# Partition sums by a high and a low fp32r product instead of one fp32 product, in a two-block transformer kernel

## What is computed

```python
def rmsnorm(x, w):                       # HGRN2: o of each head, 128 wide
    y = x32 * lax.rsqrt(jnp.mean(x32 * x32, axis=-1, keepdims=True) + EPS)

def l2norm(x):                           # GDN: q and k of each head
    return x * lax.rsqrt(jnp.sum(x * x, axis=-1, keepdims=True) + EPS)

# stick breaking: -log_stay is softplus(z), masked
later = lax.cumsum(log_stay, axis=3, reverse=True) - log_stay
weights = jnp.where(valid, jnp.exp(log_beta + later), 0.0)
```

## Time and profile before

| | us |
|---|---|
| median of 3 runs | 2780.7 (2780.24 to 2782.86) |
| profiled execution | 2784.13 |
| its span, first to last instruction | 2782.3 |
| PE busy | 2749.6 |
| VectorE busy | 1959.7 |
| ScalarE busy | 1325.1 |
| GpSimd busy | 71.4 |

### The profile page before, as it was taken

The page is one execution under the profiler, slowest core; times in us unless marked ns, Lnnn a source line. Parts: engine busy times, 40 slices in busy tenths (PEclk is TensorE's granted clock), DMA queues, the critical chain, the costliest instruction groups (busy, mean ns, idle before and its releaser), DMA issues.

```text
span 2782.3 us, 42599 instructions
## 1 busy us (share of the span) xinstructions
PE 2749.6 (99%) x15230; PEld 2370.1 (85%) x15230; DVE 1959.7 (70%) x2726; ACT 1325.1 (48%) x1656; POOL 71.4 (3%) x95
## 2 busy tenths in 40 slices
PE   8999999999999999999999999999999999999998
PEld 7888888887888888888878888888888888888887
DVE  6777777768888888644465677757578888885444
ACT  6444444435444444433365555566454444443443
POOL 0000000010000000000000000000000000000000
PEclk9999999999999999999999999999999999999999
DMA  6544444454555555665545533345455555555554
GB/s 231 173 154 163 153 159 153 153 160 149 186 190 199 186 181 189 189 191 187 189 133 175 167 130 128 123 149 184 144 180 183 192 190 181 192 193 189 187 182 151
DMA packets 132883, 479.28 MB, mean 172 GB/s; under 512 B 14720, under 2 KB 16912, under 8 KB 132640
## 3 DMA queue, kind: packets, MB, share of 16 engines
q1 hardware_dynamic: 132144, 474.15, 51.6%
q0 software_dynamic: 624, 3.53, 0.4%
HBM read 475.53 MB, written 2.10 MB: 172 GB/s over the span
## 4 chain that ended last, share of the span: by engine, by line
PE 77%; DVE 10%; issue 5%; DMA 4%; ACT 3%; DVEq 1%; ACTq 0%; SPq 0%
PE acc L397 26%; PE acc L399 13%; PE acc L420 8%; PE acc L422 8%; PE acc L421 8%; DMA raw<-stream 4%; PE acc L369 4%; DVE wts L320 4%; ACT wts L314 2%; PE ps L1209 2%; PE acc L371 2%; DVE cy L1974 2%; DVE cin L347 1%; DVE half L339 1%; PE ps L1732 1%
## 5 line engine op out<-in xcount | busy, mean ns | idle before, releaser
L397 PE MATMUL acc<-hs,wts 128*128 128x512 f32 x4672 | 1651.6, 396 | 5.2 <-DVE wts L320 2.7
L320 DVE TENSOR_TENSOR wts<-raw,wts 128x1024 fp32r<-128x1024 f32 x896 | 1069.5, 1224 | 607.3 <-ACT wts L314 607.1
L314 ACT ACTIVATE wts<-raw 128x1024 fp32r<-128x1024 f32 x896 | 921.7, 1054 | 920.3 <-PE acc L399 406.5
L399 PE MATMUL acc<-hs,wts 128*128 128x256 f32 x4672 | 1308.1, 280 | 0.0
L397 PEld LDWEIGHTS acc<-hs,wts 128*128 128x128 f32 x4672 | 879.8, 188 | 201.5 <-issue 6.8
L399 PEld LDWEIGHTS acc<-hs,wts 128*128 128x128 f32 x4672 | 880.1, 188 | 2.2 <-issue 2.2
L420 PE MATMUL acc<-wts,acts 128*128 128x512 f32 x704 | 279.1, 396 | 0.9 <-DVE wts L320 0.8
L422 PE MATMUL acc<-wts,acts 128*128 128x512 f32 x704 | 279.1, 396 | 0.0
L421 PE MATMUL acc<-wts,acts 128*128 128x512 f32 x704 | 276.7, 393 | 0.0
L328 ACT ACTIVATE half<-acc 128x512 f32<-128x512 f32 x162 | 96.1, 593 | 169.3 <-PE acc L399 150.3
L420 PEld LDWEIGHTS acc<-wts,acts 128*128 128x128 f32 x704 | 132.2, 188 | 32.9 <-DVE wts L320 2.2
(11 more groups left out here) (318 smaller groups left out, 2182.3 us busy)
## 6 DMA issues: line engine op xcount, KB each, us to landing
raw<-stream SPq DMA_DIRECT2D x896, 512.0 KB, 3.8
xf<-xT SPq DMA_DIRECT2D x4, 512.0 KB, 7.6
memr<-memT POOLq DMA_DIRECT2D x1, 2048.0 KB, 8.8
outT<-memr SPq DMA_DIRECT2D x4, 256.0 KB, 2.3
outT<-memr SPq DMA_DIRECT2D x2, 512.0 KB, 3.8
KQ<-masks POOLq DMA_DIRECT2D x1, 448.0 KB, 6.1
vec<-vecs POOLq DMA_DIRECT2D x1, 352.0 KB, 6.4
cst<-consts POOLq DMA_DIRECT2D x1, 256.0 KB, 5.9
```

Of the source, the lines that this page charges most:

```text
L314: nc.scalar.activation(whi[:, b, :], raw[:, b, :], ACT.Copy).then_inc(hi_ready, 1)
L320: nc.vector.tensor_tensor(wlo[:, b, :], raw[:, b, :], whi[:, b, :].bitcast(F32), ALU.subtract).then_inc(lo_ready, 1)
L397: nc.tensor.matmul(acc[:, 2 * par + n, :], whi[:, b, c:c + P], src[:, kt, :], start=start, stop=False)
L399: mm = nc.tensor.matmul(acc[:, 2 * par + n, 0:T], wlo[:, b, c:c + P], src[:, kt, 0:T], start=False, stop=stop)
```

## The change

Every sum named above is made by two fp32r products that add up in the accumulator, of a high part (rounded to fp32r) and a low part (the rest).

- HGRN: ScalarE squares twice, into `out_sq` and, rounded, into `sqh`. VectorE subtracts one from the other (`sql`), in a step of its own, in its third step. PE's sum goes two steps later and waits for `sql`; Ln and Exp and VectorE's scaling go one step of their engines later. `out_rms` lies where `sqh` lies.
- Stick breaking: ScalarE copies softplus, rounded (`spp[:, 0]`), VectorE subtracts (`spp[:, 1]`). The sums are in another layout: bank 0 holds the 256 columns of both heads, bank 1 the last 128 of both, so that one product serves two heads. VectorE's subtraction from `zm` becomes two instructions. All from the sums on goes one block later.
- GDN: ScalarE squares a second time, rounded (`gsh`), behind the first square and ahead of the table of Ln. VectorE subtracts (`gsl`) as the first instruction of the head's work. PE's sums go one step later and wait for that; the k by k product stays in its step.
- The constants are copied once to fp32r (`ones_r`, `sums_r`).

```diff
@@ hg_vector_out
-            yield from pause(3)
+            yield from pause(2)
+            dve.wait_ge(hg_act_out.sem, hg_act_out.count("sqh", turn))
+            nc.vector.tensor_tensor(sql, out_sq, sqh.bitcast(F32),
+                                    ALU.subtract).then_inc(hg_vec_out.sem, 1)
+            yield from pause(2)
             dve.wait_ge(hg_act_out.sem, hg_act_out.count("or", turn))
@@ hg_scalar_out
             nc.scalar.activation(out_sq, ps[:, 0, :], ACT.Square).then_inc(hg_act_out.sem, 1)
-            yield
+            nc.scalar.activation(sqh, ps[:, 0, :], ACT.Square).then_inc(hg_act_out.sem, 1)
+            yield from pause(2)
@@ hg_tensor_out
-            yield from pause(4 if last else 2)
-            pe.wait_ge(hg_act_out.sem, hg_act_out.count("osq", turn))
-            nc.tensor.matmul(ps[:, 2, :], ones, out_sq, start=True, stop=True).then_inc(hg_pe_out.sem, 1)
+            yield from pause(6 if last else 4)
+            pe.wait_ge(hg_vec_out.sem, hg_vec_out.count("sql", turn))
+            nc.tensor.matmul(ps[:, 2, :], ones_r, sqh, start=True, stop=False)
+            nc.tensor.matmul(ps[:, 2, :], ones_r, sql, start=False, stop=True).then_inc(hg_pe_out.sem, 1)
@@ sb_tensor
             yield from pause(9)
-            pe.wait_ge(sb_vec.sem, sb_vec.count("sp", t))
-            for h in range(2):
-                nc.tensor.matmul(ps[:, h, 0:T], row_ge, sp_[:, h, 0:T], start=True, stop=False)
-                nc.tensor.matmul(ps[:, h, P:T], ones, sp_[:, h, T:T + P], start=False, stop=True)
-                mm = nc.tensor.matmul(ps[:, h, T:T + P], row_ge, sp_[:, h, T:T + P], start=True, stop=True)
+            yield from pause(2)
+            pe.wait_ge(sb_vec.sem, sb_vec.count("spl", t))
+            now = ps[:, 0, :].rearrange("p (h n) -> p h n", h=2)
+            for s in range(2):
+                nc.tensor.matmul(now, sums_r[:, 1], spp[:, s, :, 0:T], start=(s == 0), stop=False)
+                nc.tensor.matmul(now[:, :, P:T], sums_r[:, 0], spp[:, s, :, T:T + P], start=False, stop=(s == 1))
+                mm = nc.tensor.matmul(ps[:, 1, 0:T], sums_r[:, 1], spp[:, s, :, T:T + P], start=(s == 0), stop=(s == 1))
@@ sb_scalar
-            yield from pause(5)
+            yield from pause(2)
+            act.wait_ge(sb_vec.sem, sb_vec.count("sp", t))
+            nc.scalar.activation(spp[:, 0], sp_[:], ACT.Copy).then_inc(sb_act.sem, 1)
+            yield from pause(4)
@@ sb_vector
-            yield from pause(3)
+            yield from pause(2)
+            dve.wait_ge(sb_act.sem, sb_act.count("sph", t))
+            nc.vector.tensor_tensor(spp[:, 1], sp_[:], spp[:, 0].bitcast(F32), ALU.subtract).then_inc(sb_vec.sem, 1)
+            yield from pause(2)
@@ gd_vector
             flat = "p a b -> p (a b)"
+            dve.wait_ge(gd_act_in.sem, gd_act_in.count("sqh", t))
+            nc.vector.tensor_tensor(gsl[:], gs[:], gsh[:].bitcast(F32), ALU.subtract).then_inc(gd_vec.sem, 1)
             dve.wait_ge(gd_pe.sem, gd_pe.count("rows", t))
@@ gd_scalar_in
             nc.scalar.activation(gs[:], gy[:, 0:2, :].rearrange("p a b -> p (a b)"), ACT.Square).then_inc(gd_act_in.sem, 1)
+            if t:
+                act.wait_ge(gd_vec.sem, gd_vec.count("q", t - 1))
+            nc.scalar.activation(gsh[:], gy[:, 0:2, :].rearrange("p a b -> p (a b)"),
+                                 ACT.Square).then_inc(gd_act_in.sem, 1)
             nc.scalar.preload_act_table(ACT.Ln)
@@ gd_tensor
-            pe.wait_ge(gd_act_in.sem, gd_act_in.count("sqk", t))
+            yield
+            pe.wait_ge(gd_vec.sem, gd_vec.count("sql", t))
...
             for b in range(2):
-                mm = nc.tensor.matmul(ps[:, b, :], ones, gs[:, b * 2 * T:(b + 1) * 2 * T], start=True, stop=True)
+                part = slice(b * 2 * T, (b + 1) * 2 * T)
+                nc.tensor.matmul(ps[:, b, :], sums_r[:, 0], gsh[:, part], start=True, stop=False)
+                mm = nc.tensor.matmul(ps[:, b, :], sums_r[:, 0], gsl[:, part], start=False, stop=True)
             mm.then_inc(gd_pe.sem, 1)
...
-            yield from pause(4)
+            yield from pause(3)
             pe.wait_ge(gd_vec.sem, gd_vec.count("k", t))
```

More of the change, by code:

```diff
@@ L158, in build @@
             KM = sb("KM", [P, 2, 2 * T], F32, st)
-            osr = sb("osr", [P, 2, 2 * T], F32, st)
+            out_sq = sb("out_sq", [P, 2 * T], F32, st)[:]
+            with ExitStack() as st2:
+                out_rms = sb("out_rms", [P, 2 * T], F32, st2)[:]
+            sqh = sb("sqh", [P, 2 * T], F32R, st)[:]
+            sql = sb("sql", [P, 2 * T], F32R, st)[:]
+            ones_r = sb("ones_r", [P, P], F32R, st)[:]
             AD = sb("AD", [P, 4, P], F32, st)
@@ L172, in build @@
             tls = sb("tls", [P, 2, DT, 16], F32R, st)
+            sums_r = sb("sums_r", [P, 2, P], F32R, st)
             with ExitStack() as st2:
@@ L179, in build @@
                 svn = sb("svn", [P, 4, P], F32, st2)
+                spp = sb("spp", [P, 2, 2, 384], F32R, st2)
             with ExitStack() as st2:
                 gy = sb("gy", [P, 3, 2 * T], F32, st2)
-                gs = sb("gs", [P, 4 * T], F32, st2)
-                gr = sb("gr", [P, 4 * T], F32, st2)
+                with ExitStack() as st3:
+                    gs = sb("gs", [P, 4 * T], F32, st3)
+                    gr = sb("gr", [P, 4 * T], F32, st3)
+                gsl = sb("gsl", [P, 4 * T], F32R, st2)
+                gsh = sb("gsh", [P, 4 * T], F32R, st2)
                 vb = sb("vb", [P, 4, P], F32, st2)
@@ L266, in build @@
         hg_pool = Steps(sem("hg_pool"), names("k0 k1 k2 k3 k4 k5 k6"))
-        hg_act_out = Steps(sem("hg_act_out"), names("osq oln or"))
+        hg_act_out = Steps(sem("hg_act_out"), names("osq sqh oln or"))
         hg_vec = Steps(sem("hg_vec"), names(
@@ L270, in build @@
             "lo5 up5 c4 w6 lo6 up6 c5 lo7 up7 c6"))
-        hg_vec_out = Steps(sem("hg_vec_out"), names("og os hi lo"))
+        hg_vec_out = Steps(sem("hg_vec_out"), names("sql og os hi lo"))
         hg_pe = Steps(sem("hg_pe"), names("diag g0 g1 g2 g3 g4 g5 g6 l128"))
@@ L279, in build @@
         gt_pe = Steps(sem("gt_pe"), names("both lg cum"))
-        sb_act = Steps(sem("sb_act"), names("abs e l w hi"))
-        sb_vec = Steps(sem("sb_vec"), names("zm sp w lo"))
+        sb_act = Steps(sem("sb_act"), names("abs e l sph w hi"))
+        sb_vec = Steps(sem("sb_vec"), names("zm sp spl w0 w lo"))
         sb_pe = Steps(sem("sb_pe"), names("z cs o"))
-        gd_act_in = Steps(sem("gd_act_in"), names("silu sqk"))
+        gd_act_in = Steps(sem("gd_act_in"), names("silu sqk sqh"))
         gd_act = Steps(sem("gd_act"), names(
@@ L288, in build @@
         gd_vec = Steps(sem("gd_vec"), names(
-            "d k q Tm TT nl0 nl tt0 at0 at qd t0 t1 tt1 t2 tt2 t3 tt3 t4 tt4 t5 tt5 tt6 S"))
+            "sql d k q Tm TT nl0 nl tt0 at0 at qd t0 t1 tt1 t2 tt2 t3 tt3 t4 tt4 t5 tt5 tt6 S"))
         gd_pool = Steps(sem("gd_pool"), names("z1 z2 z3 z4 z5 z6"))
@@ L959, in first_vector @@
                                   KQ[:].rearrange("p a b -> p (a b)")[:, 0:LEVELS * P])
+            dve.wait_ge(cst_in, 16)
+            nc.vector.tensor_copy(ones_r, ones)
             yield
@@ L1138, in hg_vector @@
                 yield
-        out_sq, out_rms = osr[:, 0], osr[:, 1]
         def hg_vector_out(dve, turn, par):
             n = hin[:, par]
-            yield from pause(3)
+            yield from pause(2)
[3 more added lines that the diff above has]
+            yield from pause(2)
             dve.wait_ge(hg_act_out.sem, hg_act_out.count("or", turn))
@@ L1366, in gate_vector @@
             yield
+            nc.vector.tensor_copy(sums_r[:], cst[:, 1:3, :])
             dve.wait_ge(gt_act.sem, gt_act.count("egc"))
@@ L1477, in sb_vector @@
             nc.vector.scalar_tensor_tensor(sp_[:], zm[:], 0.0, se[:], ALU.max, ALU.add).then_inc(sb_vec.sem, 1)
-            yield from pause(3)
+            yield from pause(2)
+            dve.wait_ge(sb_act.sem, sb_act.count("sph", t))
+            nc.vector.tensor_tensor(spp[:, 1], sp_[:], spp[:, 0].bitcast(F32), ALU.subtract).then_inc(sb_vec.sem, 1)
+            yield from pause(2)
             dve.wait_ge(sb_pe.sem, sb_pe.count("cs", t))
-            nc.vector.tensor_tensor(zm[:], zm[:], ps[:, 0:2, 0:384], ALU.subtract).then_inc(sb_vec.sem, 1)
+            nc.vector.tensor_tensor(zm[:, :, 0:T], zm[:, :, 0:T], ps[:, 0, :].rearrange("p (h n) -> p h n", h=2),
+                                    ALU.subtract).then_inc(sb_vec.sem, 1)
+            nc.vector.tensor_tensor(zm[:, :, T:T + P], zm[:, :, T:T + P],
+                                    ps[:, 1, 0:T].rearrange("p (h n) -> p h n", h=2),
+                                    ALU.subtract).then_inc(sb_vec.sem, 1)
             yield from pause(3)
```

## The result

The changed kernel takes 2810.85 us (median of 4, 2809.2 to 2814.81), against 2780.91 for the kernel before (median of 4, the runs beside it included). The ratio is 1.0106, 95% interval 1.0094 to 1.0118. It is 29.9 us slower; forecast was 2807, with 2796 to 2820 as the range. The profiled execution took 2814.81, its span is 2813.0.

What follows compares the result with a forecast made beforehand. PE, busy 99% of the span, was taken as the bound; +20.8 (GDN) + 8.8 (clock) + 0.3 (HGRN) - 3.3 (stick breaking) = +26.6 us, giving 2810.7 profiled, 2807.4 median, range 2796 to 2820.

Steps and rivals of the forecast that it cites:

- Work saved: PE's sums in HGRN, GDN and stick breaking: fp32r products cheaper than fp32, 9.7 us saved in all.
- The GDN stall: GDN sums: PE waits for VectorE's queued subtraction, 5.30 us at the first head pair, 24.6 us over four.
- The clock: PE behind each of four GDN stalls: half clock costs 2.2 us each, 8.8 us in all.
- the 1.5 us of waits for the scaled k: GDN k by k product: 0.5 us wait at three of four heads, counted only at full clock.
- Sum of GDN: GDN part: 20.8 us net of stalls and savings plus 8.8 us of low clock.
- the 2.3 us of a low stretch: GDN: some 2.3 of each 6.7 us low-clock stretch falls into the stall itself, where it costs nothing.
- HGRN: HGRN sums over eight head pairs: waits for the subtraction against cheaper products, +0.3 us net; bounds -4 and +2.
- six waits: HGRN sums, first six head pairs: 0.45 us waited for the subtraction, 0.40 saved, +0.05 net each.
- the seventh: HGRN's seventh head pair: PE waits 1.57 us because VectorE splits two blocks first, net +1.2.
- The eighth pair's -1.2: HGRN's eighth head pair: an existing 0.8 us wait for a weight split goes and 0.4 is saved.
- Stick breaking: Stick-breaking sums: cheaper products and no new wait, -3.3 us; +1 as a bound if longer copies delay a split.
- signs of being wrong: Profile signs: no or short GDN sum wait, waits moved to HGRN masked products, fp32r sums over 0.25 us apart.

Runs made afterwards that it cites:

- sb_only: Kernel before with only the stick-breaking part of the change: ratio 0.9986, 3.9 us faster than the kernel before.
- hg_apart: hg_spread with VectorE's scaling chain one step later for the first six HGRN head pairs too: ratio 0.9979 to the kernel before, -5.8 us.
- gd_early: The change with VectorE's GDN subtraction some 6 us earlier and PE's sums one step later: ratio 1.0017 to the kernel before, +4.7 us.
- gd_filled: The change with 40 small constant products ahead of PE's wait in each GDN head pair: ratio 1.0083 to the kernel before, +23.1 us.
- hg_spread: The change without GDN; HGRN sums one step later for six pairs, two for the seventh, whose scaling chain moves two: 0.9985 of the kernel before.

## Why the prediction came out right, step by step

- **Work saved.** 9.7 us from distances between starts; sb_only and hg_apart show 3.3 and 3.2 of it where no wait is in the way.
- **The GDN stall.** Right in place, cause and size. The sum had 6.44 us for the second head pair; it is 6.30 (1684.76 to 1691.06), since the second square adds 0.97 between starts, not 1.08. At the first it is 5.2, for 5.3. gd_early shows that order made it: 24.8 us of 29.5 go with it.
- **The clock.** Right that each of the four stalls brings a low stretch; three of 6.8 us and one of 10.2. The Trainium skill (TensorE: Matmul & The Clock Gate, Part 1) has the rule that activity releases the half rate. These four stretches and gd_filled, where products fill the wait and the clock stays at 2.4 GHz, agree with it. The size was too small, though 8.8 estimated and 9.1 measured look alike, for they are not the same thing. The 8.8 stands in a sum without the 1.5 us of waits for the scaled k, and the 9.1 is what is left after such waits are hidden. At full clock the prediction's terms for GDN give 20.8 + 1.5 = 22.3, and gd_filled has 22.3. Its clock term then adds 29.6 - 22.3 = 7.3 net, where 9.1 was measured.
- **Sum of GDN.** 29.6 predicted, 31.4 measured. The 1.8 are that difference. The step at fault is the 2.3 us of a low stretch that were taken to fall into the stall. The first three begin at 1615.0, 1690.1 and 1765.2, and PE's sums at 1616.15, 1691.06 and 1766.04, so 0.8 to 1.1 us fall into it and nearly 6 us hit products, not 4.4. At the fourth, 1836.9 against 1841.08, 4.2 us fall into it, but that stretch is the long one.
- **HGRN.** +0.3 predicted, +2.6 measured: the step with an effect missing. Two terms were too small: six waits cost 0.17 net instead of 0.05, the seventh 1.3 instead of 1.2. One was put at nothing: "It delays the first masked product's keys by some 1 us; PE had no wait there". The room there was 1.2 us at the ordinary pairs (keys ready at 224.9, product at 226.1), so it held, with 0.2 to spare (226.1 and 226.3 in the change). At the eighth pair the room was the same, but the whole chain of 2.6 us comes ahead of the keys, and there was 1.4 us of wait by the starts. The eighth pair, the kernel before and then the change:

```profile
557.17 0.67 POOL L2166 COPY KM<-KQ 128x512 f32<-128x512 f32 x1 [12.43 <-DVE KQ L1131]
559.09 1.13 PE L1209 MATMUL ps<-KQ,KM 128*128 128x128 f32 x8
...
557.97 0.74 DVE L1162 SCALAR_TENSOR_TENSOR out_sq<-ps,vec,out_rms 128x512 f32<-128x512 f32 x1
560.54 0.69 DVE L1142 TENSOR_TENSOR KQ<-KQ,sig 128x512 f32<-128x512 f32 x1
561.89 0.67 POOL L2204 COPY KM<-KQ 128x512 f32<-128x512 f32 x1 [16.25 <-DVE KQ L1143]
562.61 1.23 PE L1224 MATMUL ps<-KQ,KM 128*128 128x128 f32 x8 [1.17 <-POOL KM L2204]
```

  hg_spread shows that the chain's place made it. No wait in a trace doesn't say how much room there is; I had read it as if it did. The eighth pair's -1.2 came out at -1.16.
- **Stick breaking.** -3.3 predicted and measured.

The errors of +1.8 and +2.3 make up the 4.1 us between the forecast for the profiled execution, 2810.7, and its 2814.8; the median stands 3.4 above the forecast for it, which by the prediction's own terms is 2807.3, not 2807.4. Two of the signs of being wrong showed although the main path was right: a wait at a masked product of HGRN (1.2 us in the list), and fp32r sums spaced by more than 0.25 us, 0.43 at half clock and 0.34 behind a wait.

## To carry to other kernels

On an engine that never waits, an instruction that waits for a busy engine costs its whole wait, and what counts is not how long the producer takes but what stands ahead of it in its queue: here 1.2 us of subtraction cost PE 5.2 us once and about 6.3 us three times. Put the producer of such an operand where its engine idles, ahead of bulk work, and only then move the user. And before moving steps, measure the room between each product and what it needs, as a wait that is not there can be 0.2 us away.

## What the runs showed that I had not expected

- The first product behind a wait starts 0.34 us ahead of the next instead of 0.23 (PE's timeline of the change, HGRN sums):

```profile
213.81 0.50 PE L1257 MATMUL ps<-sqh,ones_r 128*128 128x512 f32 x1 [0.30 <-DVE sql L1156]
214.15 0.39 PE L1258 MATMUL ps<-sql,ones_r 128*128 128x512 f32 x1
```

  That is 0.11 us a wait, and most of the difference between 0.05 and 0.17. The constant is loaded only after the wait, though it was ready (timeline of PE's weight loads):

```profile
213.81 0.19 PEld L1257 LDWEIGHTS ps<-sqh,ones_r 128*128 128x128 f32 x1 [0.61 <-DVE sql L1156]
```

  In the kernel the wait stands ahead of both the load and the product. The Trainium skill (the same page, Part 2, step 1) has weight loads pulled ahead of products; over a wait in front of the load itself this trace doesn't show it.
- Waits of 1.7, 1.9 and 1.9 us were followed by a low clock once, for 3.4 us (gd_early); four of 5.2 to 6.3 us were followed by 6.8 or 10.2. What decides between them stays open.
